# Samples' index scores and key search moved into the joint program of a hybrid attention and state-space layer, with earlier first loads and the key rows spread over more steps

## The reference, cut to what matters

```python
h = _rmsnorm(x, g_pre) * (1.0 + scale) + shift
z = h @ w_in          # q 8x128, k/v 2x128, iq 16x64, ik 64, iw 16, za 1024, u 1024, zs 1024
s = jnp.einsum('bqhd,bsd->bqhs', iq, ik) * (IDX_DIM ** -0.5)
score = jnp.einsum('bqhs,bqh->bqs', jax.nn.relu(s), iw)
_, idx = lax.top_k(score, topk)        # topk = min(256, n_keys // 4)
...
logits = jnp.einsum('bqhgd,bqnhd->bqhgn', qg, kg) * (HEAD_DIM ** -0.5)
o = jnp.einsum('bqhgn,bqnhd->bqhgd', jax.nn.softmax(logits), vg)
attn = attn * jax.nn.silu(za)
y_ssm = jax.nn.gelu(y_ssm)             # of the S5 scan
y_ssm = y_ssm * jax.nn.sigmoid(y_ssm @ w_glu + b_glu) * jax.nn.silu(zs)
y = x + gate * _rmsnorm(concat([attn, y_ssm]) @ w_out, g_post)
```

## Time and profile before

| what | value |
|---|---|
| median of 3 runs | 2333.34 us (2328.88 to 2334.1) |
| the profiled execution's own time | 2342.47 us |
| its span | 2340.7 us |
| PE busy | 2132.5 us, 91% |
| DVE, ACT, POOL busy | 1254.3, 719.2, 317.5 us |
| projection | 0 to 1417 us |
| joint program | 1422.2 to 1753.9 us |
| samples' program | 1753.9 to 1855.6 us |
| output projection | 1855.6 to 2340.7 us |

### The profile page before, as it was taken

One profiled execution on the slowest core, in us unless ns is written; L12 is line 12 of the kernel. 1 busy time (PEld: TensorE's weight loads), 2 busy tenths in 40 slices (PEclk: granted clock), 3 DMA queues, 4 the chain that ended last, 5 costly groups with the idle time before them and its releaser, 6 DMA issues. The chain is left out here.

```text
span 2340.7 us, 33431 instructions
## 1 busy us (share of the span) xinstructions
PE 2132.5 (91%) x12705; PEld 1885.6 (81%) x12705; DVE 1254.3 (54%) x2489; ACT 719.2 (31%) x1406; POOL 317.5 (14%) x591
## 2 busy tenths in 40 slices
PE   5898888999999999999999994889996899998896
PEld 4678787888899999999999994778773668875784
DVE  6555564444324888888776662666653252224224
ACT  5331122111134333333332212455441242221321
POOL 0253442555300000000000000000001200004001
PEclk9999899999999999999999996999996599999997
DMA  9963356555443333333333426543203222226335
GB/s 354 340 152 92 109 131 159 157 181 174 135 105 86 95 97 91 91 94 94 92 93 96 102 58 188 175 124 115 82 23 84 81 65 79 74 81 212 97 96 175
DMA packets 361355, 288.39 MB, mean 123 GB/s; under 512 B 108217, under 2 KB 302977, under 8 KB 359913
## 3 DMA queue, kind: packets, MB, share of 16 engines
q1 hardware_dynamic: 335506, 249.35, 38.5%
q10 hardware_dynamic: 24368, 33.18, 4.3%
q0 software_dynamic: 1328, 3.80, 0.5%
HBM read 226.06 MB, written 60.20 MB: 122 GB/s over the span
## 5 line engine op out<-in xcount | busy, mean ns | idle before, releaser
L1281 PE MATMUL ps_z<-h_hi,w_hi 128*128 128x384 f32 (+2 forms) x1936 | 666.1, 344 | 0.0
L1283 PE MATMUL ps_z<-h_hi,w_lo 128*128 128x384 f32 (+2 forms) x1936 | 656.5, 339 | 0.0
L1282 PE MATMUL ps_z<-h_lo,w_hi 128*128 128x384 f32 (+2 forms) x1936 | 656.5, 339 | 0.0
L1281 PEld LDWEIGHTS ps_z<-h_hi,w_hi 128*128 128x128 f32 (+1 forms) x1936 | 362.9, 187 | 15.8 <-issue 5.5
L1282 PEld LDWEIGHTS ps_z<-h_lo,w_hi 128*128 128x128 f32 (+1 forms) x1936 | 363.0, 187 | 5.0
L1283 PEld LDWEIGHTS ps_z<-h_hi,w_lo 128*128 128x128 f32 (+1 forms) x1936 | 362.6, 187 | 5.3
L865 DVE TENSOR_TENSOR w_lo<-w_raw,w_hi 128x512 fp32r<-128x512 f32 (+1 forms) x172 | 122.3, 712 | 356.2 <-ACT w_hi L531 354.5
L2619 DVE TENSOR_TENSOR o_lo<-o_raw,o_hi 128x512 fp32r<-128x512 f32 x128 | 90.2, 706 | 282.8 <-ACT o_hi L2575 282.6
L531 ACT ACTIVATE w_hi<-w_raw 128x512 fp32r<-128x512 f32 (+1 forms) x172 | 107.5, 627 | 258.5 <-DMA w_raw<-in_w_in 198.9
L2575 ACT ACTIVATE o_hi<-o_raw 128x512 fp32r<-128x512 f32 x128 | 81.1, 634 | 312.2 <-PE ps_out L2760 248.7
L997 DVE MAX8 top<-score 128x8 f32<-128x1024 f32 (+5 forms) x192 | 171.0, 891 | 3.4
(11 more groups left out here) (432 smaller groups left out, 3179.3 us busy)
## 6 DMA issues: line engine op xcount, KB each, us to landing
w_raw<-in_w_in SPq DMA_DIRECT2D x176, 256.0 KB, 3.1
wada<-in_w_ada SPq DMA_DIRECT2D x32, 1024.0 KB, 9.1
o_raw<-in_w_out SPq DMA_DIRECT2D x128, 256.0 KB
wg<-in_w_ada SPq DMA_DIRECT2D x32, 512.0 KB, 5.0
zt<-z_sb ACTq DMA_DIRECT2D x28, 576.0 KB, 4.3
g_raw<-in_w_glu SPq DMA_DIRECT2D x24, 512.0 KB, 4.3
xs<-in_x_prompt SPq DMA_DIRECT2D x8, 1024.0 KB, 7.7
iq_raw<-zt SPq DMA_DIRECT2D x48, 128.0 KB, 3.3
```

Of the source, the lines that this page charges most:

```text
L1281: M(to, w_hi[q][:, k, 0:m], h_hi[:, kk, cols], start=kk == 0, stop=False)
L1282: M(to, w_hi[q][:, k, 0:m], h_lo[:, kk, cols], start=False, stop=False)
L1283: return M(to, w_lo[q][:, k, 0:m], h_hi[:, kk, cols], start=False, stop=kk == KB - 1)
```

## The change

**First loads.** In `project_in`, at step 172 of 180, SP also issues the loads of the joint program's first query tiles (`q`, tiles 0 and 1) and of the first 128 columns of keys and values (`kv_first`). The joint program takes its first logits from `kv_first`; its queue begins with the index keys and `za`, and loads `kT` and `vT` whole, one DMA of 1,152 KB each, in place of 256 KB first and 896 KB later.

**Rows spread.** The key rows of tile t are turned in the steps of `ROW_STEP`: 0, 1, 3, 4, 6, 7, 9, 10, 12.

**Index scores.** In the joint program, SP's queue loads the samples' index queries after step 9, in 8 DMAs of pieces of 64 bytes (16 positions of 4 bytes), and the cached index keys two samples at a time. PE turns the cached keys of sample b at steps 14, 16, ... 28 (`turn_cached`), computes one of the 16 parts (sample, half of the heads) in each of steps 15 to 30 (`index_part`), and adds it into one PSUM bank in the next step (`index_sum`). ACT copies the turned keys (`index_keys`), DVE rectifies each part (`rectified`). The scores are read at DVE's step 32 and the 9 rounds of the search follow, one a step, in steps 33 to 41. The sum's bank is the one that `beside` used, so that only the unit U = 1 still has it.

**Buffers.** `g_raw` has 2 buffers instead of 3, and the load of `v_raw` for the second block stands at step 14 instead of 9.

**Samples' inputs.** At step 45 SP's queue loads the samples' queries (8 DMAs of 64-byte pieces), `za` and the first two samples' cached keys. The samples' program begins with its attention. The gate is built there by ACT (tanh, and a copy at half scale) and DVE; before, POOL did it.

The diff, cut to its core:

```diff
+            def load_next():
+                sp.wait_ge(s_mm, 8 * PIECES)
+                sp.wait_ge(z_out, stored_before[29])
+                for t in range(2):
+                    sp.dma_start(q_first[:, t], zt[Q0:K0, t * P:t * P + P].rearrange("(h d) t -> d h t", d=HD)).then_inc(next_in, 16)
+                sp.dma_start(kv_first[:], zt[K0:IQ0, 0:P].rearrange("(h d) t -> d h t", d=HD)).then_inc(next_in, 16)
...
+                if S == starts[-1] + 4:
+                    load_next()
+            sp.wait_ge(next_in, 16 * 3)
...
+    ROW_STEP = [3 * t // 2 for t in range(NT)]
+    INDEX_AT = ROW_STEP[-1] + 3
+    BLK = PAST // P
+    HP = IDX_HEADS // 2
+    INDEX_PARTS = 2 * DEC_B
+    SEARCH_ROUNDS = DEC_TOPK // 8 + 1
...
+        q, kv_first = keep["q"], keep["kv_first"]
+        iq = nc.alloc_sbuf_tensor_at("iq_s", [P, DEC_B, HP * DEC_S], F32, offset=keep["back_base"] + 17408)
...
-        for i in range(3):
+        for i in range(2):
...
-        beside = [U % 2 == 1 and ends[U] + 2 < WIDE for U in range(GLU)]
+        beside = [U % 2 == 1 and ends[U] + 2 < INDEX_AT for U in range(GLU)]
...
-                if U >= 3:
-                    sp.wait_ge(g_pass, 3 * (U - 3) + 2)
+                if U >= 2:
+                    sp.wait_ge(g_pass, 3 * (U - 2) + 2)
                 i = U % NB
-                sp.dma_start(w_raw[U % 3][:], wv[:, :, i * P:i * P + P]).then_inc(w_in[U % 3], 16)
+                sp.dma_start(w_raw[U % 2][:], wv[:, :, i * P:i * P + P]).then_inc(w_in[U % 2], 16)
...
+            def load_index():
+                sp.wait_ge(logits_mm, HEADS)
+                sp.wait_ge(kv_T, 1)
+                for b in range(DEC_B):
+                    at = SEQ + DEC_S * b
+                    sp.dma_start(iq[:, b].rearrange("p (a t) -> p a t", t=DEC_S),
+                                 zt[IQ0:IK0, at:at + DEC_S].rearrange("(a q) t -> q a t", q=P)).then_inc(iq_in, 16)
...
+            def load_samples():
+                sp.wait_ge(g_pass, 3 * NB * 2)
+                for b in range(2):
+                    sp.dma_start(cached[:, b], io["cache_k"][0, b].rearrange("(n p) h d -> p n (h d)", p=P)).then_inc(samples_in, 16)
+                for b in range(DEC_B):
+                    at = SEQ + DEC_S * b
+                    sp.dma_start(q_pre[:, b].rearrange("p (h t) -> p h t", t=DEC_S), zt[Q0:K0, at:at + DEC_S].rearrange("(h d) t -> d h t", d=HD)).then_inc(samples_in, 16)
+                sp.dma_start(za_pre[:], zt[ZA0:U0, SEQ:TOK].rearrange("(h d) t -> d h t", d=HD)).then_inc(samples_in, 16)
...
             sp.dma_start(ikT[:], zt[IK0:IW0]).then_inc(ik_in, 16)
             load_za(0)
-            load_keys(1, FIRST_KEYS, TOK)
-            load_values(1, FIRST_KEYS, TOK)
+            sp.dma_start(kT[:], zt[K0:V0].rearrange("(h d) t -> d h t", d=HD)).then_inc(k_in, 16)
+            sp.dma_start(vT[:], zt[V0:IQ0].rearrange("(h d) t -> d h t", d=HD)).then_inc(vT_in, 16)
             load_w(0)
             load_v(0)
             load_w(1)
-            load_z(0)
-            load_block(0)
-            load_q(1)
-            load_z(1)
-            load_block(1)
-            load_w(2)
+            for U in range(2):
+                load_z(U)
+                load_block(U)
             load_z(2)
+            load_index_rows()
+            for b in range(2):
+                load_cached_index(b)
...
+                if n == HEADS + 1:
+                    load_index()
+                if n >= INDEX_AT and cached_at(n - 1) is not None and cached_at(n - 1) + 2 < DEC_B:
+                    load_cached_index(cached_at(n - 1) + 2)
+                if n == ends[2 * NB - 1] + 1:
+                    load_samples()
...
-                if n < NT:
-                    value_rows(n)
+                if n in ROW_STEP:
+                    value_rows(ROW_STEP.index(n))
+                if cached_at(n) is not None:
+                    index_keys(cached_at(n))
...
+            def rectified(e):
+                b, h2 = divmod(e, 2)
+                dve.wait_ge(s_mm, e + 1)
+                if e == 0:
+                    dve.wait_ge(once_ok, 3)
+                if e >= 2:
+                    dve.wait_ge(sum_mm, e - 1)
+                V.tensor_scalar(rel[:, h2], ps_l[0][:, 512:512 + DEC_KEYS], 0.0, wcol[:, h2, b:b + 1],
+                                ALU.max, ALU.mult).then_inc(rel_ok, 1)
...
-                if 1 <= n <= NT:
-                    key_rows(n - 1)
+                if n - 1 in ROW_STEP:
+                    key_rows(ROW_STEP.index(n - 1))
+                if n == INDEX_AT - 1:
+                    index_once()
+                if n == INDEX_AT:
+                    index_weights()
+                if part_at(n - 1) is not None:
+                    rectified(part_at(n - 1))
+                if n == WIDE:
+                    index_scores()
+                if 0 <= n - WIDE - 1 < SEARCH_ROUNDS:
+                    search(n - WIDE - 1)
...
+            def index_part(e):
+                b, h2 = divmod(e, 2)
+                half = slice(64 * h2, 64 * h2 + 64)
+                pe.wait_ge(ik_ok, 2 * b + 2)
+                if e == 0:
+                    pe.wait_ge(iq_in, 16 * DEC_B)
+                    pe.wait_ge(once_ok, 3)
+                else:
+                    pe.wait_ge(rel_ok, e)
+                M(ps_l[0][:, 512:512 + DEC_KEYS], iq[half, b], ikT_s[half, b % 2], start=True, stop=True).then_inc(s_mm, 1)
+
+            def index_sum(e):
+                b, h2 = divmod(e, 2)
+                pe.wait_ge(rel_ok, e + 1)
+                if e == 0:
+                    pe.wait_ge(g_sig, last_beside + 1)
+                M(ps_l[1][:, 512:512 + DEC_KEYS], pick[:, 112 - DEC_S * b:240 - DEC_S * b], rel[:, h2], start=e == 0,
+                  stop=e == INDEX_PARTS - 1).then_inc(sum_mm, 1)
...
             logits(0)
             for n in range(N + 1):
-                if n < NT:
-                    turn_rows(n)
+                if n in ROW_STEP:
+                    turn_rows(ROW_STEP.index(n))
                 if n + 1 < N:
                     logits(n + 1)
+                if n == INDEX_AT - 1:
+                    turn_weights()
+                if cached_at(n) is not None:
+                    turn_cached(cached_at(n))
+                if part_at(n - 1) is not None:
+                    index_sum(part_at(n - 1))
+                if part_at(n) is not None:
+                    index_part(part_at(n))
...
-            for b in range(DEC_B):
-                idx_keys(b)
-            act.wait_ge(once_in, 16 * 5)
+            keys(0)
             A(gate[:], za[:], ACT.Tanh, scale=0.5).then_inc(sig_ok, 1)
-            keys(0)
+            act.wait_ge(sig_ok, 1)
+            A(za[:], za[:], ACT.Copy, scale=0.5).then_inc(sig_ok, 1)
...
+            V.tensor_copy(spread[:], bc(ident[:].rearrange("p (b t) -> p b t", t=DEC_S), 2, HEADS)).then_inc(spread_ok, 1)
+            dve.wait_ge(sig_ok, 2)
+            V.scalar_tensor_tensor(gate[:], gate[:], 1.0, za[:], ALU.add, ALU.mult).then_inc(gate_ok, 1)
```

More of the change, by code:

```diff
@@ L1636, in v_rows, with part_at, cached_at @@
             return v_nat[:, t] if t < TILES else v_last[:]
-        FIRST_KEYS = 2 * P
+        def part_at(n):
+            return n - INDEX_AT if 0 <= n - INDEX_AT < INDEX_PARTS else None
+        def cached_at(n):
+            b, odd = divmod(n - INDEX_AT + 1, 2)
+            return b if not odd and 0 <= b < DEC_B else None
         block = ctx.enter_context(nc.Block())
@@ new lines, in load_index_rows, with load_cached_index @@
+            def load_index_rows():
+                for half in range(2):
+                    sp.dma_start(ik_new[64 * half:64 * half + 64, :], zt[IK0:IW0, SEQ:TOK]).then_inc(ik_new_in, 16)
+                src = zt[IW0:IW0 + IDX_HEADS, SEQ:TOK].rearrange("(a h) (b t) -> h b a t", h=2, b=DEC_B)
+                for h2 in range(2):
+                    sp.dma_start(w_rows[DEC_B * h2:DEC_B * h2 + DEC_B], src[h2]).then_inc(w_rows_in, 16)
+            def load_cached_index(b):
+                if b >= 2:
+                    sp.wait_ge(ik_T, b - 1)
+                src = io["cache_idx_k"][0, b].rearrange("(n p) d -> p n d", p=P)
+                for twice in range(2):
+                    sp.dma_start(ik_cached[:, b % 2, :, twice], src).then_inc(ikc_in[b % 2], 16)
@@ L1693, in _ @@
             load_w(1)
-            load_z(0)
-            load_block(0)
-            load_q(1)
-            load_z(1)
-            load_block(1)
-            load_w(2)
+            for U in range(2):
+                load_z(U)
+                load_block(U)
             load_z(2)
+            load_index_rows()
+            for b in range(2):
+                load_cached_index(b)
             for n in range(N):
-                for U in range(3, GLU):
-                    if piece_step[3 * (U - 3) + 1] == n:
+                for U in range(2, GLU):
+                    if piece_step[3 * (U - 2) + 1] == n:
                         load_w(U)
@@ L1807, in _ @@
```

(15 more changed lines are left out.)

278 lines of the change are left out of this document (108 added, 170 removed).

## The result

The changed kernel took **2305.31 us** in the median of 4 runs (2300.58 to 2313.74), the kernel before 2333.72 (2328.88 to 2336.61): ratio 0.9882, 95% interval 0.9858 to 0.9905. Timed again on another occasion, beside its own runs of the kernel before (2333.76 in the median), it took **2300.98 us** (2294.96 to 2303.16): ratio 0.9852, interval 0.9833 to 0.9871. Forecast: 2300, range 2284 to 2316. It is faster, by 28 to 33 us.

The account below looks back on a forecast made before the run. PE was busy 91% of the span, and each program's end is set by its own chain, so terms add: -8 + 15 + 0.5 - 41.5 = -34.0. From 2333.3 that gives 2299.5, said as 2300; range 2284 to 2316.

Parts of the forecast that it names:

- Start and rows, -8: Joint program's start: early first loads and spread key rows remove waits for loads and stores, -8 us, bounds -4 and -12.
- Index scores, +15: Joint program, steps 14 to 31: 20.0 us of PE work, 6.0 hidden in waits, 1.0 for the shared bank; +15 us.
- Search, +0.5: Joint program, nine steps: DVE's search rounds mostly fit its idle time, +0.5 us; +9 if nothing hides them.
- Samples' program, -41.5: Samples' start: first turn 6.6 us after the program's first instruction instead of 48.1, loop unchanged; -41.5 us.
- The rest: Projection's last weight loads behind the new loads, and two buffers of g_raw for three: taken as 0.
- the clock of the samples' loop: Rival: the samples' loop keeps full clock, about 15 us more gained, 2284 us; chance 0.13.
- the start did give its gain: Rival denied here: vT lands as late as before, stalls move on, first term 0, 2307 us; chance 0.07.
- small pieces: Rival: loads of 64-byte pieces hold up SP's queue ahead of the GLU's weights, 2340 us; chance 0.04.
- The first rival: Joint program: index work unhidden, rectified parts late, search delays probs; +30 instead of +15.5, 2314 us; chance 0.14.

Follow-up runs that it names:

- before_spread: Kernel before with only the key rows spread over steps 0, 1, 3, 4, 6, 7, 9, 10, 12; turn(13) at 60.0 us, 10.9 us earlier.
- index_thin: Changed kernel with index parts 1 to 15 and sums 1 to 14 of 16 columns instead of 272; turn(13) to turn(32) took 94.1 us.
- pieces_twice: Changed kernel with the samples' index queries loaded twice; turn(13) came 5.8 us later, turn(32) 8.9 us.
- rectify_late: Changed kernel with DVE rectifying each part after its step's normalising instead of before; turn(13) to turn(32) took 124.2 us, 24.5 longer.

## Why the prediction was right

The forecast was -34.0 us; the stretches that the change touches gave -32.3 in the first profile and -33.7 in the second (333.8 - 326.0 in the joint program, -41.5 after it). The mechanism held in each stretch, but the sum is this close in part by luck: the start gave 1.4 to 2.8 us more than forecast and the index scores cost 3.6 more, and these nearly cancel. The medians lie 5 and 1 us from the 2300 forecast, and 4 us from each other.

- **Start and rows, -8.** Measured -9.4 and -10.8. Turn(1) was forecast 15.0 us after the start and came at 15.0 and 14.4, turn(4) at 23.8 and came at 24.7 and 23.9. That `vT` as a whole is due next, and that the wait is only moved, held. So did the spreading, which is the whole gain: alone in the kernel before it gave 10.9. With it goes the clock, which the sum left out: it came back to 1.00 at 48.3 us before, at 37.0 and 35.6 in the changed kernel and at 34.5 in before_spread; how much of the gain that is was not separated. The early loads, which the sum counted as +1.0 with the wider pieces, are a wash. Two slips in the working did no harm: its items add up to -8.6 and not -8, and what moved away from ahead of `vT` is 1,024 KB and not 1,280 (the second query tile stood behind it), though the 3,104 KB that it works with are right.
- **Index scores, +15.** The term was too small by 3.6. Matmuls: 21.4 us from start to start (parts 10.7, sums 8.5, cached keys 2.0, weights 0.2) where 20.0 stood. Hidden: waits fell from 9.8 to 6.8, so 3 and not 6. The lost banks, taken as 1.0, were 2.8 alone in the kernel before, part of them at a half clock that the changed kernel doesn't have there. The sum also left out what the clock gave back: 3.4 us at 0.50 in step 26 before and none after, up to 1.7 us. These overlap and don't add up exactly. index_thin shows the same from the other side: only 3.8 of 9.6 us were hidden.
- **Search, +0.5.** Measured 0.0 (174.0 and 174.0), although DVE works 7.4 us more there.
- **Samples' program, -41.5.** Measured -41.5, the first turn after 6.5 us and the loop unchanged at clock 0.50. The path was the one that the sum walks: keys copied, tanh, copy at half scale, DVE's product (1774.01 to 1775.23), then the maximum.
- **The rest.** The last weights of the projection did not wait for the new loads: the w_hi rows of both profiles keep their distance (6.1 to 6.4 us) from 700 us on to the end. The +6.2 us before the joint program stood there at 174 us already (5.2), in code that is the same, while the second profile stood 0.8 apart there and began the joint program 3.7 earlier: scatter. What makes it was not looked into.

Of the rivals, the clock of the samples' loop did not come back, the start did give its gain, and one set of small pieces cost nothing. Their margin was thinner than the prediction had it, which pieces_twice shows. The first rival's price for the joint program, 30 us in place of 15.5, is what a wrong place on DVE costs (rectify_late), not what this order does.

## What to carry to other kernels

Work moved from an idle program into a busy one costs its full length on the engine that bounds it, less what waits it fills; here 3 of 21 us fell into waits, for a gain of 41 where it came from. Work in such a wait can also go with a clock that stays full in the next step, so a comparison of stretches needs the clock beside the waits. A load taken ahead helps only as far as the next load that the same step needs, so follow the queue to its second and third wait before pricing it. Where one engine's operation stands ahead of everything else in its step, the place of its partner on the other engine matters more than its length: 16 operations of 0.5 us moved behind one other cost 24.5 us, some 15 of them as more waiting and the rest at half clock.
